# The opening of a two-block transformer kernel: all eight modulation blocks as one-column products on TensorE

## The reference, cut to what matters

```python
ada = (c @ w_ada + b_ada)[:, None, :]                 # c: (1, 1024), w_ada: (1024, 6144)
shift1, scale1, gate1, shift2, scale2, gate2 = jnp.split(ada, 6, axis=-1)
h = rmsnorm(x, g_norm1) * (1.0 + scale1) + shift1     # x: (1, 256, 1024)
proj = h @ w_in                                       # then attention, branches, MLP, second block
```

## Time and profile before

| What | Value |
|---|---|
| median of three runs | 1083.36 us |
| profiled execution, device time | 1082.66 us |
| its span, first to last instruction | 1080.9 us |
| TensorE busy with products | 1041.5 us (96%) |
| VectorE, ScalarE, GpSimd busy | 649.0, 546.4, 362.9 us |
| `w_hi` of a unit (L1277), mean | 1909 ns |
| `w_lo` of a unit (L1856), mean | 2469 ns |
| HBM read | 195.03 MB, 181 GB/s over the span |

### The profile page before, as it was taken

One profiled execution on the slowest core, in us unless ns is written; L12 is line 12 of the kernel. 1 busy time (PEld: TensorE's weight loads), 2 busy tenths in 40 slices (PEclk: granted clock), 3 DMA queues, 4 the chain that ended last, 5 costly groups with the idle time before them and its releaser, 6 DMA issues.

```text
span 1080.9 us, 19685 instructions
## 1 busy us (share of the span) xinstructions
PE 1041.5 (96%) x8492; PEld 1011.9 (94%) x8492; DVE 649.0 (60%) x834; ACT 546.4 (51%) x768; POOL 362.9 (34%) x192
## 2 busy tenths in 40 slices
PE   2999999999999999999999999999999989999998
PEld 1699999999999999999999999999898889999998
DVE  5867668666765654637865454445857756444444
ACT  2477767744656444564345344343754545444441
POOL 4028368330545433450302342221433212242231
PEclk9999999999999999999999999999999999999999
DMA  9988587536576655533546555566533145555531
GB/s 329 303 266 254 174 286 237 192 118 197 183 257 222 196 177 174 195 117 118 171 152 210 172 194 179 172 202 198 148 110 109 49 147 178 192 181 191 177 136 40
DMA packets 169859, 197.37 MB, mean 183 GB/s; under 512 B 5379, under 2 KB 137900, under 8 KB 169644
## 3 DMA queue, kind: packets, MB, share of 16 engines
q1 hardware_dynamic: 169772, 196.11, 56.1%
HBM read 195.03 MB, written 1.06 MB: 181 GB/s over the span
## 4 chain that ended last, share of the span: by engine, by line
PE 84%; DVE 7%; ACT 3%; DMA 2%; POOL 2%; issue 1%; SPq 0%; DVEq 0%; ACTq 0%; POOLq 0%
PE bank L516 83%; DVE w_lo L1856 3%; DMA ada_raw<-in_w_ada 1%; ACT w_hi L1277 1%; DMA xT<-in_x 1%; ACT ada_raw L1267 1%; PE bank L759 1%; POOL big L1716 0%; ACT h_hi L1371 0%; DVE big L2321 0%; DVE head_bias L2409 0%; DVE fresh L2184 0%; DVE big L2310 0%; POOL qk L1716 0%; POOL probs L1716 0%
## 5 line engine op out<-in xcount | busy, mean ns | idle before, releaser
L1856 DVE TENSOR_TENSOR w_lo<-w_raw,w_hi 128x2048 fp32r<-128x2048 f32 x158 | 389.5, 2469 | 244.5 <-ACT w_hi L1277 243.5
L516 PE MATMUL bank<-h_hi,w_hi 128*128 128x256 f32 x1328 | 371.6, 287 | 5.2 <-DVE w_lo L1856 2.4
L1277 ACT ACTIVATE w_hi<-w_raw 128x2048 fp32r<-128x2048 f32 x158 | 301.4, 1909 | 139.4 <-PE bank L516 132.3
L516 PE MATMUL bank<-h_hi,w_lo 128*128 128x256 f32 x1328 | 366.4, 283 | 0.0
L516 PE MATMUL bank<-h_lo,w_hi 128*128 128x256 f32 x1328 | 345.3, 283 | 0.0
L516 PE MATMUL bank<-u_hi,w_hi 128*128 128x256 f32 x1040 | 294.1, 286 | 4.4 <-DVE w_lo L1856 2.0
L516 PE MATMUL bank<-u_hi,w_lo 128*128 128x256 f32 x1040 | 291.6, 284 | 0.0
L516 PE MATMUL bank<-u_lo,w_hi 128*128 128x256 f32 x1040 | 282.5, 284 | 0.0
L1671 POOL TENSOR_TENSOR u_lo<-fresh,u_hi 128x512 fp32r<-128x512 f32 x60 | 142.4, 2375 | 416.3 <-ACT u_hi L1286 416.2
L516 PEld LDWEIGHTS bank<-h_hi,w_hi 128*128 128x128 f32 x1328 | 253.5, 192 | 11.3 <-issue 6.9
L516 PEld LDWEIGHTS bank<-h_hi,w_lo 128*128 128x128 f32 x1328 | 253.6, 192 | 0.0
(11 more groups left out here) (264 smaller groups left out, 962.8 us busy)
## 6 DMA issues: line engine op xcount, KB each, us to landing
w_raw<-in_w_mlp SPq DMA_DIRECT2D x32, 1024.0 KB, 5.4
w_raw<-in_w_up SPq DMA_DIRECT2D x32, 1024.0 KB, 5.4
w_raw<-in_w_down SPq DMA_DIRECT2D x32, 1024.0 KB, 5.0
w_raw<-in_w_in SPq DMA_DIRECT2D x21, 1024.0 KB, 6.5
ada_raw<-in_w_ada SPq DMA_DIRECT2D x19, 1024.0 KB, 7.8
w_raw<-in_a_w_in SPq DMA_DIRECT2D x10, 1024.0 KB, 5.1
w_raw<-in_w_o SPq DMA_DIRECT2D x8, 1024.0 KB, 5.1
w_raw<-in_w_out SPq DMA_DIRECT2D x4, 1024.0 KB, 5.1
```

Of the source, the lines that this page charges most:

```text
L516: return pe.matmul(dst, lhsT, rhs, start=start, stop=stop, skip_group_check=True)
L1277: act.activation(w_hi[:, n % PARTS_RING, :], w_raw[:, slot_of[n], :], ACT.Copy).then_inc(hi_w, 1)
L1856: dve.tensor_tensor(w_lo[:, n % PARTS_RING, :], w_raw[:, slot_of[n], :], w_hi[:, n % PARTS_RING, :].bitcast(F32), ALU.subtract).then_inc(l ...
```

## The change

`ada_direct` replaces `ada_unit` of VectorE, the way by ScalarE and GpSimd of block 3, `ada_rows` and `ada_block`: the block itself is the stationary operand, a column of `c` the moving one, and four row tiles are accumulated. That is 16 products of one column for a block, 128 for the eight. Blocks 0 to 5 go to `ps_ada` and 6 and 7 to another bank. With blocks 0 to 5 the first twelve columns are there, enough for the first four tiles of `h`; blocks 6 and 7 give the last four. Unit 0 is cut into those halves, with block 7 in between. Units 1 and 2 make all products with `w_hi` first. All low halves of `h` are now made on VectorE, and the seven warm-up products become five, between blocks 5 and 6.

```diff
             def load_unit(n):
...
-                elif n == 1:
-                    sp.wait_ge(ada_vector, 4)
-                elif n == 2:
-                    sp.wait_ge(ada_used, 1)
-                elif n == 3:
-                    sp.wait_ge(ada_vector, 5)
+                elif n in (1, 2, 3):
+                    sp.wait_ge(ada_used, 4 + n)
...
+            def ada_direct(a):
+
+                tiles, dst, at = ada_tiles(a), ps_ada if a < 6 else acc[1], 4 * (a // 2) if a < 6 else 0
                 ada_in(pe, a)
                 for kt in range(4):
+                    scale = vec[:, V_C + 4 * (a % 2) + kt:V_C + 4 * (a % 2) + kt + 1]
+                    for c in range(4):
+                        last = mm(dst[:, at + c:at + c + 1], tiles[:, kt, c * P:c * P + P], scale,
+                                  a in (0, 6) and kt == 0 and c == 0, a % 2 == 1 and kt == 3)
                 last.then_inc(ada_used, 1)
...
+            pe.wait_ge(vec_in, 16)
+            for a in range(4):
+                ada_direct(a)
             pe.wait_ge(consts_in, 16)
-            pe.wait_ge(ada_vector, 2)
-            ada_block(0, ada_part[:, 0, :])
             sum_x("sum1")
...
             def first_unit():
 
+                pe.wait_ge(hi_w, N_IDX + 1)
+                first_pairs((0, 1), "hh")
+                ada_direct(7)
+                first_pairs((0, 1), "hl")
+                pe.wait_ge(lo_w, N_IDX + 1)
+                first_pairs((0, 1), "lh")
+                first_pairs((2, 3), "hh")
+                first_pairs((2, 3), "lh")
+                first_pairs((2, 3), "hl").then_inc(unit_done, 1)
...
+                elif n <= N_IDX + 2:
+                    product_lo_last(n)
...
+            act.wait_ge(ada_ready, 2)
+            first_hi((0, 1))
             split_w(0)
-            act.wait_ge(ada_used, 1)
-            act.activation(ada_row, acc[1][0:1, :], ACT.Copy).then_inc(ada_copied, 1)
...
+            act.wait_ge(ada_ready, 4)
+            first_hi((2, 3))
             split_w(1)
             split_w(2)
...
+                dve.wait_ge(ada_used, 4 + 2 * done)
+                dve.tensor_tensor(ada[:, at], src, vec[:, V_ADA + at.start:V_ADA + at.stop], ALU.add).then_inc(ada_ready, 1)
...
+            first_ada(1, slice(0, 12), ps_ada[:, 0:12])
+            first_h((0, 1))
+            first_lo((0, 1))
             split_w(0)
...
+            first_ada(2, slice(12, 16), acc[1][:, 0:4])
+            first_h((2, 3))
+            first_lo((2, 3))
             split_w(1)
             split_w(2)
```

More of the change, by code:

```diff
@@ L801, in _, with first_pairs @@
             mm(ps_misc[0:HEADS, 0:384], rel[0:33, :], buckets[0:33, :], True, True).then_inc(misc_full, 1)
+            ada_direct(4)
             spread_sum(1, acc[0])
[L803 to L817, removed]
+            ada_direct(5)
+            keep_busy(WARM)
+            ada_direct(6)
+            def first_pairs(pairs, which):
                 wh, wl = (t[:, 0, :].rearrange("p (k n) -> p k n", k=KT) for t in (w_hi, w_lo))
-                def pair(q, w, x, last):
+                w, x = {"hh": (wh, h_hi), "lh": (wl, h_hi), "hl": (wh, h_lo)}[which]
+                for q in pairs:
+                    pe.wait_ge(h1_lo if which == "hl" else h1_hi, q + 1)
                     for kt in (2 * q, 2 * q + 1):
@@ L823, in pair, with first_unit, product_lo_last @@
                             ins = mm(lin[0][:, nt * T:nt * T + T], w[:, kt, nt * P:nt * P + P], x[:, kt, :],
[L824 to L834, removed]
+                                     which == "hh" and kt == 0 and nt == 0, which == "hl" and kt == 7)
+                return ins
+            def first_unit():
+                pe.wait_ge(hi_w, N_IDX + 1)
[7 more added lines that the diff above has]
+                first_pairs((2, 3), "hl").then_inc(unit_done, 1)
+            def product_lo_last(n):
+                wh, wl = (t[:, n % PARTS_RING, :].rearrange("p (k n) -> p k n", k=KT) for t in (w_hi, w_lo))
+                pe.wait_ge(hi_w, n + 1)
+                if before[n]:
+                    user, value = before[n]
+                    pe.wait_ge(evac_a if user == "a" else evac_v, value)
+                for kt in range(KT):
+                    for nt in range(2):
+                        for x in (h_hi, h_lo):
+                            mm(lin[lin_bank[n]][:, nt * T:nt * T + T], wh[:, kt, nt * P:nt * P + P], x[:, kt, :],
+                               kt == 0 and nt == 0 and x is h_hi, False)
+                pe.wait_ge(lo_w, n + 1)
+                for kt in range(KT):
+                    for nt in range(2):
+                        last = mm(lin[lin_bank[n]][:, nt * T:nt * T + T], wl[:, kt, nt * P:nt * P + P], h_hi[:, kt, :],
+                                  False, kt == KT - 1)
+                last.then_inc(unit_done, 1)
             for n in range(N_IDX, N_GF):
@@ L2003, in _ @@
             dve.tensor_tensor(vec[:, V_MIX:V_MIX + 8], vec[:, V_MIX:V_MIX + 8], vec[:, V_GF:V_GF + 8], ALU.mult)
-            for a in (0, 1, 2):
-                ada_unit(a)
             mean_square("sum1")
@@ new lines, in first_h, with first_lo @@
+            def first_h(pairs):
+                for q in pairs:
+                    for i in range(2):
+                        k = 2 * q + i
+                        last = dve.tensor_scalar(h1_pairs[q][:, i * T:i * T + T], x_hat[:, k, :], gs[:, 0, k:k + 1], ada[:, k:k + 1],
+                                                 ALU.mult, ALU.add)
+                    last.then_inc(h1_ready, 1)
+            def first_lo(pairs):
+                for q in pairs:
+                    dve.wait_ge(h1_ready, q + 1)
+                    dve.wait_ge(h1_hi, q + 1)
+                    dve.tensor_tensor(flat(h_lo, 2 * q, 2 * q + 2), h1_pairs[q], flat(h_hi, 2 * q, 2 * q + 2).bitcast(F32),
+                                      ALU.subtract).then_inc(h1_lo, 1)
```

107 lines of the change are left out of this document (21 added, 86 removed).

## The result

The changed kernel takes 1109.28 us (median of four runs, 1108.86 to 1110.52) and the kernel before in the same job 1083.68 (1082.98 to 1089.38): a ratio of 1.0232, 95% interval [1.0216, 1.0249], slower. 1109.0 was predicted, with a range of 1098 to 1117. The profiled execution took 1108.86 us, its span is 1106.7.

What follows compares the result with a forecast made beforehand. VectorE's modulation passes were taken to fill the opening before TensorE's nearly unbroken work; with TensorE setting it, unit 1 starts 25.3 us later: 1082.66 + 25.3 = 1108.0, plus 0.7 from profiled run to median, 1109, range 1098 to 1117.

Steps and rivals of the forecast that it cites:

- Steps 1 to 4: TensorE's blocks 0 to 5 as one-column products at half clock, 6.8 us each, plus small sums, ending at 51.5.
- Step 5: Five warm-up products behind block 5: clock back after 4.4 us, 6.4 us in all, to 57.9.
- Step 6: Block 6, eight products of unit 0's first half, then block 7: 3.6, 1.0 and 6.0 us, to 68.5.
- Step 7: Rest of unit 0: low halves 3.4 us, second half 3.4; unit 1 starts at 75.3 instead of 49.98.
- The queue of loads: Weights 1 to 4 wait longer on SP; put at nothing, at most a load's 8.7 us if it bound.
- what follows: Behind unit 1's start engines keep their distances to TensorE; none of its 19.4 us idle shrinks.
- Paid back in part: Rival: a quarter of the later 19.4 us idle vanishes behind the longer opening, 5 less, 1104; chance 0.09.
- No change by a warm engine: Rival: one-column products warm TensorE, blocks take 3.6 us, opening 49.8 against 49.98, time 1083; chance 0.11.
- Cheaper products: Rival: weight loads overlap more, the last block's arrival sets the opening's end at 38.7, 11 less, 1072; chance 0.04.

Runs made afterwards that it cites:

- clock raised ahead: Changed kernel with four useless 512-column products on TensorE ahead of block 0: 1107.31 us, ratio 1.0214 to the kernel before.
- three quarters left out: Changed kernel with only one of four row tiles of blocks 0 to 5 multiplied: 1085.6 us, ratio 1.0010 to the kernel before.
- shared openings: Kernel before with unit 0 in halves and modulation blocks shared among VectorE, ScalarE with GpSimd, and TensorE; four variants: 1085.62, 1083.79, 1082.97, 1082.39 us.
- the last two shared openings: The second shared opening without its two late warm-up products, then also without the middle one: 1082.97 us (ratio 0.9982) and 1082.39 us (0.9981).
- the run above: Changed kernel with blocks 0 to 5 as 512-column moving operand, columns of c as weights, sums not turned into columns: 1096.32 us, ratio 1.0115.
- second shared opening: Against the kernel before: blocks 5 and 7 on TensorE as wide rows of sums, five on VectorE, 3 on ScalarE and GpSimd: 1083.79 us, ratio 0.9995.
- first shared opening: Against the kernel before: blocks 5 and 6 on TensorE as one-column products, five on VectorE, 3 on ScalarE and GpSimd: 1085.62 us, ratio 1.0014.
- the kernel with wide products between: Changed kernel with one useless 512-column product behind each of the first three row tiles of blocks 0 to 5: 1141.02 us, ratio 1.0526.

## Why the prediction was right

**Steps 1 to 4, the price and the clock (to 51.5; measured 51.03).** The mechanism was right: 6.8 us a block, as worked out from two small groups of the earlier trace rows. The end comes 0.5 us early because block 0's data did, at 6.58 instead of 7.09. What I had read from one fall at 35.45 was shown by the kernel with the clock raised ahead; the one with three quarters left out shows these products as all of the loss but 0.8 us. The Trainium skill, "TensorE: Matmul & The Clock Gate", Part 1, says that sustained matmul activity releases the throttle; taken as time in which TensorE has matmuls to run, this case disagrees with it: 37.15 busy of 37.40 us at 0.50.

**Step 5, the warm-up (6.4; measured 6.07).** The clock was full from 54.5, 3.4 us after the passes began, where I had taken 4.4.

**Step 6, blocks 6 and 7 (3.6, 1.0 and 6.0; measured 3.5, 1.3 and 6.7).** Here a size was off. I let the full clock last 5.5 us from block 6's start; it lasted 4.2 (57.1 to 61.3), so the whole of block 7 ran at 0.2125 us a load. The first eight products of unit 0 lost a part of their time too.

**Step 7 (75.3; measured 74.75).** The first two pairs' low halves took 3.3 us against 3.4. The clock was back at 71.5 instead of 73.0, so the second half took 2.9 instead of 3.4. ScalarE had `w_hi` of unit 1 at 73.0 (72.9 predicted). The errors of steps 1 and 5 to 7 are of both signs (0.5 and 0.3 us early, 0.9 late, 0.6 early) and leave 0.55 us.

**The queue of loads and what follows.** Nothing of the queue was seen in a bracket before unit 1. I let the shift from there to the end stay as it was, and here a term was put at nothing that is not: the rest is 1.03 us longer, with 1.4 us more of products and 0.4 less idle. The same products, found in both traces behind the same pauses, show where. They are 24.77 us apart at unit 1 and 25.73 at 221.34 (247.07 in the changed kernel, which at 207.99 waits 0.78 us for ScalarE as the kernel before does not). They are 24.53 apart at 476.34 (500.87), since a wait of 1.03 us for `w_lo` at 309.81 is not there any more. Then comes a half-clock spell of 3.4 us at 501.6, and at 531.97 (557.80) and from there to the end they are 25.83 apart: the spell cost 1.30 us.

```profile
476.34 1.02 PE L516 MATMUL bank<-consts,ada_late 128*128 128x1 f32 x8 [1.97 <-POOL ada_late L1719]
```

```profile
500.87 1.16 PE L504 MATMUL bank<-consts,ada_late 128*128 128x1 f32 x8 [1.97 <-POOL ada_late L1713]
```

Both kernels come to this place with the same pause, and the clock falls in one of them; the spell at 911.2 stands behind a pause too (1.78 us, to 910.03), as the one at 885.4 does in the kernel before. "Paid back in part", 5 us of it, did not come; 1.2 us were paid back at 309.81 and more than that was lost elsewhere.

**Luck.** The median is within 0.3 us of the 1109 that was predicted. The terms are not that good: the opening came out 0.55 us too long in the prediction, what follows 1.03 too short, and single steps of the opening were off by up to 0.9.

**The rivals.** No change by a warm engine: refuted by the block prices, and again with the clock raised ahead. Cheaper products: no 32 loads in a row are closer than 0.112 us apiece in this profile (a group of eight at 829.8 us comes to 0.102). The Trainium skill, "TensorE: Matmul & The Clock Gate", "LDWEIGHTS (loading the stationary operand)", gives the number of columns over 1.2 in nanoseconds, an estimated 107 for 128 columns; the 112 of full clock are near that, the 212.5 of half clock are not.

**Where I was wrong** was behind the prediction, in the shared openings. I moved TensorE's work by its price at full clock, when the prediction had just shown that such work lowers the clock for what stands behind it.

## What to carry to other kernels

A product with a full block of weights and one moving column costs its weight loads, and a long run of them also puts TensorE at half clock, however unbroken it is: price such work at half clock, and add what the work behind it loses. (2.4 us of such products, in the last two shared openings at 40.3 and 40.7, saw no fall.) Where the same sum can be written with the large operand moving, it costs about the same at full clock (3.6 us a block) and keeps the clock up; turning the row of sums into columns comes on top, and the run above left that out. Work taken off the engine that sets a stretch is worth only the distance to the next engine: here all of VectorE's share moved to TensorE cost 25 us, and the best of four shared openings wins 2, not all of it in the opening.

## What the runs showed of the hardware

With TensorE never idle for long, the clock's fall came 2.6 us (second shared opening, 42.1 to 44.7), 3.4 (first shared opening, 24.6 to 28.0), 4.2 (the changed kernel), 5.4 (clock raised ahead) and 5.5 (three quarters left out, and the kernel before) after the start of a run of one-column products; its return came 3.3 us (clock raised ahead, 47.9 to 51.2) to 6.1 us (three quarters left out) after wide passes began. Pauses as short as 1.8 and 2.0 us (to 910.03 and 500.87 in the changed kernel) end 1.2 and 0.7 us before a fall, and the same pause of 2.0 us in the kernel before (to 476.34) has none behind it. So the same edit can meet a clock that differs by some microseconds, and a sum that rests on such a moment needs both ends. The profile's line of slices shows full clock for stretches ahead of the first change on record, as in the kernel with wide products between (PEclk 1.00, by the price 1.2 GHz); the spacing of known products tells it.
